# Hybrid attention, convolution and PEER layer on one Trainium2 core: chunk 0's last u rows in consecutive slots, its v rows from slot 12

## The reference

```python
h = x + concat(rms_norm(stick_breaking_attention(q, k, v)), conformer_conv(c)) @ w_out
      # [q|k|v|c] = rms_norm(x) @ w_in, 8 heads of 64
xn = rms_norm(h)
qh = xn @ wq                              # 8 heads x 128, halves scored against 128 keys each
v1, i1 = top_k(qh[..., :64] @ k1.T, 16); v2, i2 = top_k(qh[..., 64:] @ k2.T, 16)
top_s, pos = top_k(v1[:, None] + v2[None, :], 16)
experts = (i1 * 128 + i2)[pos]            # 8 x 16 = 128 experts of 16384 for each token
act = gelu(sum(u_tab[experts] * xn, axis=-1))
y = h + sum(softmax(top_s) * act * v_tab[experts])
```

## Time and profile before

| | |
|---|---|
| median of 3 runs | 2912.07 us (2910.17 to 2914.2) |
| span of the profiled execution | 2910.3 us (no other time of it is given) |
| TensorE busy | 2591.2 us (89%) |
| VectorE busy | 2110.6 us (73%) |
| GpSimd busy | 1986.1 us (68%) |
| ScalarE busy | 871.6 us (30%) |
| gathers through GpSimd's queue | 1073.87 MB, 91.7% of the DMA engines' time |
| memory traffic over the span | 387 GB/s on average |

### The profile page before, as it was taken

One profiled execution on the slowest core, in us unless ns is written; L12 is line 12 of the kernel. 1 busy time (PEld: TensorE's weight loads), 2 busy tenths in 40 slices (PEclk: granted clock), 3 DMA queues, 4 the chain that ended last, 5 costly groups with the idle time before them and its releaser, 6 DMA issues.

```text
span 2910.3 us, 29785 instructions
## 1 busy us (share of the span) xinstructions
PE 2591.2 (89%) x7585; PEld 1173.6 (40%) x7585; DVE 2110.6 (73%) x5267; ACT 871.6 (30%) x2022; POOL 1986.1 (68%) x2061
## 2 busy tenths in 40 slices
PE   8999979889978899799979999799988999777777
PEld 4544434433523444244523444244523445222222
DVE  5789758866887678777887778777787757744444
ACT  3223232243213421253214521264214631211111
POOL 1026566677777777777777777777777777777775
PEclk9999999999999999999999999999999999999999
DMA  6239899899999999999999999999999999999999
GB/s 239 96 127 382 331 416 369 316 402 414 419 419 419 413 419 419 409 414 409 416 416 406 411 419 419 419 392 413 419 419 399 385 419 419 415 420 419 420 419 364
DMA packets 321344, 1125.04 MB, mean 387 GB/s; under 512 B 35937, under 2 KB 43641, under 8 KB 321176
## 3 DMA queue, kind: packets, MB, share of 16 engines
q0 software_dynamic: 294912, 1073.87, 91.7%
q1 hardware_dynamic: 26264, 49.27, 4.8%
HBM read 1114.62 MB, written 8.39 MB: 386 GB/s over the span
## 4 chain that ended last, share of the span: by engine, by line
PE 41%; DMA 25%; issue 16%; POOL 12%; DVE 4%; ACT 2%; POOLq 0%; SPq 0%; ACTq 0%; DVEq 0%
PE psum L1614 21%; DMA w_kept<-in_peer_u,experts 12%; DMA ring_v<-in_peer_v,experts 10%; PE psum L514 9%; POOL w_kept L1517 7%; POOL ring_v L1517 5%; PE psum L1038 3%; PE psum L1064 3%; PE psum L1548 2%; DVE w_kept L1933 1%; PE psum L1574 1%; DMA w_kept<-in_peer_v,experts 1%; PE psum L1564 1%; DMA qT_spill<-qT_out 1%; ACT L1751 0%
## 5 line engine op out<-in xcount | busy, mean ns | idle before, releaser
L1614 PE MATMUL psum<-ring_v,diag 128*128 128x512 f32 x3364 | 1619.6, 607 | 252.6 <-DMA ring_v<-in_peer_v,experts 163.9
L1933 DVE CUSTOM_DVE_ANT_0 w_kept<-w_kept,psum 128x1024 f32<-128x1024 f32 x928 | 1125.5, 1217 | 551.2 <-DMA w_kept<-in_peer_u,experts 548.1
L1517 POOL DMA_INDIRECT w_kept<-in_peer_u,experts x928 | 898.2, 968 | 300.1 <-issue 231.4
L1517 POOL DMA_INDIRECT ring_v<-in_peer_v,experts x878 | 847.8, 966 | 327.3 <-issue 234.5
L1614 PEld LDWEIGHTS psum<-ring_v,diag 128*128 128x128 f32 x3364 | 587.1, 191 | 1058.8 <-issue 775.2
L1760 ACT ACTIVATE diag<-ident,weights 128x128 f32<-128x128 f32 x981 | 354.2, 393 | 746.9 <-PE psum L1614 589.9
L1614 PE MATMUL psum<-w_kept,diag 128*128 128x512 f32 x560 | 269.9, 604 | 37.3 <-DMA w_kept<-in_peer_v,experts 23.5
L514 PE MATMUL psum<-w_sb,xnT 128*128 128x512 f32 x640 | 283.5, 599 | 0.8 <-ACT xnT L679 0.8
L466 POOL DMA_INDIRECT w_kept<-in_peer_u,experts x96 | 90.2, 940 | 236.7 <-DVE experts L1324 184.9
L1889 DVE SCALAR_TENSOR_TENSOR acc<-conv_in,taps,acc 128x128 f32<-128x128 f32 x720 | 205.0, 346 | 0.2
L514 PEld LDWEIGHTS psum<-w_sb,xnT 128*128 128x128 f32 x640 | 120.6, 192 | 143.4 <-issue 137.7
(11 more groups left out here) (230 smaller groups left out, 1750.9 us busy)
## 6 DMA issues: line engine op xcount, KB each, us to landing
w_kept<-in_peer_u,experts POOLq DMA_INDIRECT x1024, 9.5
ring_v<-in_peer_v,experts POOLq DMA_INDIRECT x878, 9.5
w_sb<-in_w_in SPq DMA_DIRECT2D x4, 2048.0 KB, 17.6
x_in<-in_x SPq DMA_DIRECT2D x8, 512.0 KB, 6.3
w_kept<-in_w_out SPq DMA_DIRECT2D x1, 4096.0 KB, 14.8
h_res<-in_x SPq DMA_DIRECT2D x8, 512.0 KB, 6.8
w_kept<-in_peer_wq SPq DMA_DIRECT2D x2, 2048.0 KB, 10.6
wo_sb<-in_w_out SPq DMA_DIRECT2D x1, 4096.0 KB, 19.9
```

The source lines that it names most:

```text
L1517: nc.gpsimd.indirect_dma_start(slot(kind, n), None, peer_u[0] if kind == "u" else peer_v[0], bass.IndirectOffsetOnAxis(S.experts[c % 2][:, ...
L1614: last = nc.tensor.matmul(y_ps[:, j * BANK:(j + 1) * BANK], diag[:, e % DIAGS, :], slot("v", n)[:, j * BANK:(j + 1) * BANK], start=e == 0, ...
L1933: nc.vector.tensor_tensor_reduce(out=row, in0=row, in1=hn, scale=1.0, scalar=0.0, op0=ALU.mult, op1=ALU.add, accum_out=dots[:, e:e + 1]).t ...
```

## The change

The 32 late u rows of chunk 0 take one slot each from slot 0 on, where they had every second slot: slots 0 to 31 instead of 0 to 62. The v rows 0 to 107 are spread over slots 12 to 125 instead of 4 to 125. The gelu and the weights of the two heads that these u rows complete follow at slots 16 and 32 (`heads_ended`).

```diff
-    first_at = {4 + e * (SLOTS - 5) // CAUGHT: e for e in range(CAUGHT)}
+    FIRST_V = 12
+    first_at = {FIRST_V + e * (SLOTS - FIRST_V - 1) // CAUGHT: e for e in range(CAUGHT)}
...
         if c != FIRST:
             return s
-        e = EARLY + s // 2
-        return e if s % 2 == 0 and e < ROWS else None
+        e = EARLY + s
+        return e if e < ROWS else None
...
         if c == FIRST:
-            h = AHEAD + s // (2 * TOPK) - 1
-            return [h] if s and s % (2 * TOPK) == 0 and h < PH - 1 else []
+            h = AHEAD + s // TOPK - 1
+            return [h] if s and s % TOPK == 0 and h < PH - 1 else []
```

## The result

The changed kernel took 2925.69 us (median of 4 runs, 2921.15 to 2928.9), the kernel before 2913.14 us on the same chip (4 runs): ratio 1.0042, 95% interval 1.0030 to 1.0054. A second comparison, with 10 runs, gave 2922.09 us and 1.0033 (1.0023 to 1.0042). So the change costs 9 to 13 us. The forecast was +6.4 us: sign and path right, size too small. A typical execution lies between the two.

The account below looks back on a forecast made before the run. DMA bounds up to about slot 42, TensorE to the scores, VectorE to the experts, then GpSimd. Lateness of 1.9 us at the first product, 5.3 at scores, 6.6 at experts, rounded to +6.4 on 2912.07, gave 2918.5 us; range 2907 to 2925.

Parts of the forecast that it names:

- gap filled: Hand-over from projections to chunk 0: three u rows move into the DMA gap of 340 to 350, winning 3.75 us.
- VectorE leads: Rival: VectorE sets the pace from 449 to the scores; without ten dots there the end is 7.7 us early, 2904.4; chance 0.10.
- the DMA alone counts: Rival: the engines' path is no longer than before, so -3.75 to +2 us, say 2911; chance 0.25.
- To the experts: Scores to expert numbers: VectorE takes one more side row, 1.27 us; 6.6 us late, two more TensorE rows covered.
- The slots up to 31: Slots 12 to 31 take two rows each; six more rows at 1.25 us put slot 32 7.5 us late, at 436.4.
- Slot 32 to the first product: Slots 32 to 42: TensorE's 14.9 us of work sets the time, so 1.9 us late instead of 7.5, at 451.3.
- To the scores: First product to scores: two more v rows on TensorE, 3.44 us, make 66.9 us; scores 5.3 us late, at 518.2.
- the rounding to +6.4: End of the sum: +6.6 us rounded to +6.4 because the hn_next wait of 1.2 us may shrink.
- TensorE starts late and slow: Rival: first v rows run at 1.2 GHz; 3 us lag at slot 32 plus 3 from LayerNorm, 2924.5; chance 0.20.
- the LayerNorm chain: Beside slot 35 to the first product: ends at 452.3 at the latest, taken as hidden; may stick out by 3 us.

Follow-up runs that it names:

- e1: The changed kernel with the v rows from slot 4 as before, the u rows still one per slot; ratio 1.0038 to the kernel before.
- e2: The changed kernel with the u rows on every second slot as before, the v rows still from slot 12; ratio 0.9994 to the kernel before.
- e4: The kernel before with the v rows from slot 19, the u rows still on every second slot; 2905.4 us, ratio 0.9974 to the kernel before.
- e13: The changed kernel with 16 small products of zeros on TensorE in each of slots 13 to 31, 60 and 61; 2924.51 us, ratio 1.0038.
- e5: e4 with more v rows given to VectorE between slots 42 and 76 and fewer between 77 and 116; 2908.19 us, ratio 0.9987.
- e8: The changed kernel with more v rows given to VectorE between slots 42 and 76 and fewer between 77 and 116; 2921.24 us, ratio 1.0028.

## Why the prediction was wrong in size

Point by point, from H, for the two profiles of the changed kernel:

| step | forecast | measured, first and second profile |
|---|---|---|
| gap filled, v row 0 at about 373 | yes | yes, 374.45 and 371.21 (both H+179.5 or 179.6, 373.3 on the clock of the profile before) |
| first product later than before by | 1.9 | 4.7 and 2.4 |
| first product to scores | 66.9 | 68.5 and 66.9 |
| scores later by | 5.3 | 9.7 and 5.8 |
| expert numbers later by | 6.6 | 11.5 and 7.8 |
| chunk 1's u row later by | 6.4 | 12.8 and 9.0 |
| carried to the end | 1 to 1 | 13.5 and 8.0 at the end |

**What held.** The path was the one named: gathers up to the first product, TensorE up to the scores, VectorE up to the expert numbers, then every microsecond carried on. The 2 rows more on TensorE were there (89 matmuls), and VectorE had 13 side rows for 16.5 us in place of 12 for 15.25, 1.27 us for the one more, as counted. "VectorE leads" and "the DMA alone counts" were wrong: TensorE was busy for 66.3 of 68.4 us. The side rows alone, in the search of the changed kernel:

```profile
523.80:581.40 57.60, 16.52 (x13) 1.00 0.89 318
```

**The step that failed** is "To the experts", the end of the sum, in both profiles. It went from the expert numbers straight to chunk 1's u row. GpSimd has rows of v queued between the two, and with the closer table one more. In the kernel before, then in the changed one:

```profile
569.38 0.94 POOL L1517 DMA_INDIRECT ring_v<-in_peer_v,experts  x1 [0.30 <-DVE experts L1324]
570.62 1.18 POOL L1517 DMA_INDIRECT ring_v<-in_peer_v,experts  x1 [0.31 <-issue]
```

```profile
582.02 0.94 POOL L1518 DMA_INDIRECT ring_v<-in_peer_v,experts  x1 [0.31 <-issue]
583.27 1.20 POOL L1518 DMA_INDIRECT ring_v<-in_peer_v,experts  x1 [0.30 <-issue]
584.77 0.94 POOL L1518 DMA_INDIRECT ring_v<-in_peer_v,experts  x1 [0.30 <-issue]
```

From the expert numbers to the u row it is 3.4 us before and 4.6 in the first profile, with the v rows from slot 4 (e1) 3.4 again, from slot 12 (e2) 4.6, from slot 19 (e4) 5.4. That is 1.2 us of the 2.6 that the second profile is above the forecast; the search, 2.0 us longer where I allowed 1.3 for one side row, gives another 0.7, and the first product 0.5.

**The terms that were mis-sized** are "The slots up to 31" with "Slot 32 to the first product", and "To the scores". In the first profile slot 32 was 9.9 us late from H (7.5 forecast) and the stretch to the first product 15.4 us (14.9): together 2.8 us over. In the second, 0.5 over, but by two errors that cancel: slot 32 was 6.5 us late, a microsecond less than forecast, and the stretch took 16.5 us, as TensorE waited 1.3 us there for a row of v, where I had it wait for none. The stretch to the scores was 1.6 us over in the first profile and right in the second, and the difference is the lower clock behind the wait for hn_next, for which the sum has no term. I also let that wait shrink. It grew from 1.2 to 2.1 us in both profiles, and in the first the two rows of v behind it took 4.51 us (3.60 in the second), at a window clock below full:

```profile
492.01 1.91 PE L1046 MATMUL psum<-ident,hn_next 128*128 128x128 f32 x8 [2.12 <-DVE hn_next L1158]
493.71 4.51 PE L1615 MATMUL psum<-ring_v,diag 128*128 128x512 f32 x8
```

So of the 6.4 us that the first profile's u row is later than forecast, 2.8 lie ahead of the first product, 1.6 in the stretch to the scores, 0.5 in the search, 1.2 in the queued v rows and 0.2 in the rounding to +6.4. The sum also started from a median of 2912.07 us; the kernel before took 2913.14 beside the changed one.

**The rival "TensorE starts late and slow"** gave 2924.5, nearest to the first time, and its half-clock rows were in the first profile. It is not the cause as it was told: of its 6 us, 3 were to come at slot 32 and 3 from the LayerNorm chain, for which TensorE waited 0.3 us in either profile. With the clock held up no gain in time could be measured, and the second profile is slower than the forecast without these rows at slots 31 and 32. Where the lower clock did show a cost, 1.7 us behind the wait for hn_next, the rival had priced nothing. That it came nearest to the number is luck. The Trainium skill's rule that I set beside it (TensorE: Matmul & The Clock Gate, Part 1: The HAM clock gate), that the throttled clock is the default and activity releases it, fits the runs: with e13's products the clock is 1.00 in 400 to 430, without them 0.94 and 0.90. A gain in the measured time from it they do not show.

**Left open:** why the row of slot 31 lands later in some executions (TensorE waits 4.44 us for it in one profile; in the other it is there and the wait of 2.15 us is for its diagonal), how much of that the lower clock brings about, why the clock behind the wait for hn_next is low in some executions, and why the search took 0.5 to 0.7 us more than its extra row.

## What to carry to other kernels

Rows moved to fill a hole of 4 us were charged again at the place where they went: the same gathers stood earlier, but two to a slot ahead of a point on the critical path, and cost 1.25 us each there, while the later stretches they left could not use the room. Count what stands ahead of each gate on the path, at each gate, down to the last instruction queued before the one that ends the sum, and take the larger of two limits over short stretches, not over a stage. Before explaining a few microseconds of one profile, profile the same kernel again and count from a common point.

## What the runs showed of the hardware

- A gather of 128 rows of 4 KB costs GpSimd 1.24 us to issue, as much as its transfer (1.25 us at 419 GB/s). With half rows the rate fell to 314 GB/s at the same pace of gathers.
- Two profiles of the same kernel ended at 2916.2 and 2924.9 us; 3.2 us of this were there in the first 195 us already.
- Behind the same wait of 2.1 us TensorE's granted clock over the next 6 us was 0.72 in some executions and 1.00 in others, and the stretch to the scores, in which TensorE is busy almost throughout, took 68.55 to 68.57 us with the one and 66.87 to 66.89 us with the other.
- Single gathers of 7.22 and 7.79 us on GpSimd, in place of 0.94, lay inside stretches in which VectorE worked without a break, and ended 0.4 us before those did (e5, e8).
